# The recurrence's level products and solve in all four quadrants, with VectorE's order of work rearranged

## The reference, cut to what matters

```python
sa = einsum('bhvk,bhk->bhv', S, a_t)
S  = S * w_t + sa[..., None] * b_t + v_t[..., None] * k_t
y_t = einsum('bhvk,bhk->bhv', S, r_t)
```

## Time and profile before

| what | us |
|---|---|
| median of 3 runs | 1070.66 (1070.43 to 1071.26) |
| the profiled execution | 1070.18 |
| its span | 1068.4 |
| PE busy | 1039.6 (97%) |
| VectorE busy | 653.9 (61%) |
| ScalarE busy | 453.0 (42%) |

### The profile page before, as it was taken

The page is one execution under the profiler, slowest core; times in us unless marked ns, Lnnn a source line. Parts: engine busy times, 40 slices in busy tenths (PEclk is TensorE's granted clock), DMA queues, the critical chain, the costliest instruction groups (busy, mean ns, idle before and its releaser), DMA issues.

```text
span 1068.4 us, 22579 instructions
## 1 busy us (share of the span) xinstructions
PE 1039.6 (97%) x9816; PEld 823.4 (77%) x9816; DVE 653.9 (61%) x1025; ACT 453.0 (42%) x732; POOL 5.6 (1%) x10
## 2 busy tenths in 40 slices
PE   7999999999999989999999999999999999999998
PEld 5777777676777777777777767787888888888887
DVE  4569999977466665868677667664443223444322
ACT  5455555686335533443535245344432112443111
POOL 0000000000000000000000000000000000000000
PEclk9999999999999999999999999999999999999999
DMA  9912224000532110110110121322222232223230
GB/s 360 377 61 99 79 81 176 1 2 2 197 118 79 60 42 22 43 42 25 39 42 22 42 81 43 124 93 99 99 99 99 99 99 88 93 96 114 89 104 30
DMA packets 26161, 95.01 MB, mean 89 GB/s; under 512 B 2896, under 2 KB 3152, under 8 KB 25552
## 3 DMA queue, kind: packets, MB, share of 16 engines
q1 hardware_dynamic: 26064, 93.57, 25.1%
HBM read 89.36 MB, written 4.19 MB: 88 GB/s over the span
## 4 chain that ended last, share of the span: by engine, by line
PE 76%; DVE 16%; ACT 4%; issue 2%; DMA 1%; SPq 1%; POOL 0%; ACTq 0%; DVEq 0%
PE psum L857 19%; PE psum L858 18%; PE psum L859 18%; DVE work L2067 5%; PE psum L867 3%; PE psum L1310 2%; PE psum L1323 2%; DVE small_temps L2218 1%; PE psum L1045 1%; PE psum L1024 1%; PE psum L1359 1%; PE psum L1382 1%; DMA work<-weights 1%; DVE in_weights_low L2123 1%; PE psum L1110 1%
## 5 line engine op out<-in xcount | busy, mean ns | idle before, releaser
L2123 DVE TENSOR_TENSOR weights_low<-ring,weights_high 128x1024 fp32r<-128x1024 f32 x70 | 85.8, 1226 | 75.3 <-ACT weights_high L1673 75.3
L1673 ACT ACTIVATE weights_high<-ring 128x1024 fp32r<-128x1024 f32 x70 | 73.6, 1052 | 127.5 <-PE psum L859 127.5
L857 PE MATMUL psum<-normed_high,weights_high 128*128 128x512 f32 x256 | 100.2, 391 | 0.2 <-DVE weights_low L2123 0.2
L859 PE MATMUL psum<-normed_high,weights_low 128*128 128x512 f32 x256 | 99.7, 389 | 0.0
L859 PE MATMUL psum<-hidden_high,weights_low 128*128 128x512 f32 x256 | 99.7, 389 | 0.0
L858 PE MATMUL psum<-normed_low,weights_high 128*128 128x512 f32 x256 | 99.6, 389 | 0.0
L858 PE MATMUL psum<-hidden_low,weights_high 128*128 128x512 f32 x256 | 99.6, 389 | 0.0
L857 PE MATMUL psum<-hidden_high,weights_high 128*128 128x512 f32 x256 | 99.6, 389 | 0.0
L2067 DVE SCALAR_TENSOR_TENSOR work<-work,small_sb 128x512 f32<-128x512 f32 x116 | 80.2, 745 | 0.2
L1643 ACT ACTIVATE work<-psum 128x384 f32<-128x384 f32 (+1 forms) x110 | 54.1, 541 | 56.3 <-PE psum L1359 18.8
L857 PE MATMUL psum<-pair_normed_high,pair_weights_high 128*128 128x512 f32 x176 | 75.8, 431 | 0.8 <-DVE normed_low L2127 0.8
(11 more groups left out here) (320 smaller groups left out, 2102.6 us busy)
## 6 DMA issues: line engine op xcount, KB each, us to landing
ring<-weights SPq DMA_DIRECT2D x135, 512.0 KB, 3.7
work<-weights SPq DMA_DIRECT2D x10, 512.0 KB, 12.9
residual<-xT SPq DMA_DIRECT2D x4, 512.0 KB, 7.1
mixed<-weights SPq DMA_DIRECT2D x4, 512.0 KB, 7.8
residual_saved<-residual SPq DMA_DIRECT2D x8, 256.0 KB, 4.4
residual<-residual_saved SPq DMA_DIRECT2D x1, 2048.0 KB, 9.0
outT<-residual SPq DMA_DIRECT2D x8, 256.0 KB, 3.3
tables_sb<-tables SPq DMA_DIRECT2D x1, 1280.0 KB, 10.4
```

The costliest lines, as they stand in the source:

```text
L857: pe.matmul(out, wh, high(k), start=first and n == 0, stop=False)
L859: ins = pe.matmul(out, wl, high(k), start=False, stop=last and n == len(order) - 1)
L1673: act.activation(wsplit(q)[0], room_of(b), ACT.Copy).then_inc(w_high, 1)
L2123: vec.tensor_tensor(low, room_of(b), high.bitcast(F32), ALU.subtract).then_inc(w_low, 1)
```

## The change

The products of both heads of a level are issued together for the levels in `CROSSED`, head 1 into the half of its bank that head 0 doesn't write, so that four quadrants are in use; the first level is left as it was. `solve` does the same. What head 1 finds in the other half is put right by VectorE: `Y` of head 1 is written by two instructions of 64 partitions each, and `WU` of head 1 is copied out by two VectorE instructions in place of one of ScalarE. `times_inverse_both` and `solve` wait for both heads' earlier steps before they start. VectorE's steps for other pairs get new places. The plan of PSUM banks and all other PE work is unchanged.

```diff
@@ -83,6 +83,7 @@
 STEPS = NQ * QT
 MTILES = S // P
 MUNITS = 2 * MTILES
+CROSSED = (4, 8, 16, 32)
 MU_AMID, MU_BEHIND = {0: 0, 1: 2, 2: 3, 4: 5}, {0: 1, 3: 4}
 MU_SOLVE = len(MU_AMID) + len(MU_BEHIND)
 MU_CHAIN = MU_SOLVE + 1
@@ -1302,6 +1303,18 @@
                         if c == G - 1:
                             full_inc(ins, name)
 
+            def times_inverse_both(p, b):
+
+                names = [f"y{b}_{p}_{h}" for h in range(HEADS)]
+                outs = [take(name, G * C).rearrange("p (c t) -> p c t", c=G) for name in names]
+                for c in range(G):
+                    for q in range(PARITIES):
+                        for h in range(HEADS):
+                            ins = pe.matmul(outs[h][rows(q ^ h), c, :], NT[rows(1 - q), h, c, :],
+                                            XN[rows(1 - q), h, c, :], start=True, stop=True)
+                            if c == G - 1:
+                                full_inc(ins, names[h])
+
             def times_inverse(name, h):
 
                 out = take(name, G * C).rearrange("p (c t) -> p c t", c=G)
@@ -1351,15 +1364,16 @@
                             if (c, h) == (G - 1, HEADS - 1):
                                 full_inc(ins, f"mv_{p}")
 
-            def solve(p, h):
-
-                out = take(f"wu_{p}_{h}").rearrange("p (c n) -> p c n", c=G)
+            def solve(p):
+
+                outs = [take(f"wu_{p}_{h}").rearrange("p (c n) -> p c n", c=G) for h in range(HEADS)]
                 for c in range(G):
                     for q in range(PARITIES):
-                        ins = pe.matmul(out[rows(q), c, :], XT[rows(q), h, c, :], TAM[rows(q), c, h, :],
-                                        start=True, stop=True)
-                        if c == G - 1:
-                            full_inc(ins, f"wu_{p}_{h}")
+                        for h in range(HEADS):
+                            ins = pe.matmul(outs[h][rows(q ^ h), c, :], XT[rows(q), h, c, :], TAM[rows(q), c, h, :],
+                                            start=True, stop=True)
+                            if c == G - 1:
+                                full_inc(ins, f"wu_{p}_{h}")
 
             def transitions(p):
 
@@ -1436,7 +1450,10 @@
                             pe.wait_ge(x_first, p + 1)
                         else:
                             pe.wait_ge(*is_free(f"x{prev}_{p}_{h}"))
-                        times_inverse(f"y{b}_{p}_{h}", h)
+                        if b not in CROSSED:
+                            times_inverse(f"y{b}_{p}_{h}", h)
+                    if b in CROSSED:
+                        times_inverse_both(p, b)
 
                     if p == NP - 1:
                         if b == LEVELS[0]:
@@ -1483,7 +1500,7 @@
                     pe.wait_ge(*is_free(f"ta_{p}"))
                     pe.wait_ge(*is_free(f"mv_{p}"))
                     pe.wait_ge(*is_free(f"xf_{p}_{h}"))
-                    solve(p, h)
+                solve(p)
                 if p + 1 < NP:
                     for x, lo, hi in BESIDE_CHAIN[0]:
                         project_part(beside_chain(p, x), lo, hi)
@@ -2004,8 +2021,7 @@
                 if p == NP - 1:
                     act.wait_ge(*is_free(f"gg_{NP - 2}"))
                     mixed_high(NP - 2)
-                for h in range(HEADS):
-                    copy_out(f"wu_{p}_{h}", WU[:, :, h, :], src=bank(f"wu_{p}_{h}").rearrange("p (c n) -> p c n", c=G))
+                copy_out(f"wu_{p}_0", WU[:, :, 0, :], src=bank(f"wu_{p}_0").rearrange("p (c n) -> p c n", c=G))
                 if p + 2 < NP:
                     pair_inputs(p + 2)
                 else:
@@ -2598,13 +2614,16 @@
                     mean_rest(p - 1)
                 late = p + 1 if p and p + 1 < NP else None
                 for b in LEVELS:
-                    if p + 1 < NP and b == LEVELS[2]:
-                        pair_input(p + 1, "v")
                     for h in range(HEADS):
                         name = f"y{b}_{p}_{h}"
                         vec.wait_ge(*is_full(name))
-                        free_inc(vec.tensor_tensor(Y[:, h], bank(name, G * C).rearrange("p (c t) -> p c t", c=G),
-                                                   mask(f"m{b}", G), ALU.mult), name)
+                        y, m = bank(name, G * C).rearrange("p (c t) -> p c t", c=G), mask(f"m{b}", G)
+                        if h == 0 or b not in CROSSED:
+                            ins = vec.tensor_tensor(Y[:, h], y, m, ALU.mult)
+                        else:
+                            for half in range(2):
+                                ins = vec.tensor_tensor(Y[rows(half), h], y[rows(1 - half)], m[rows(1 - half)], ALU.mult)
+                        free_inc(ins, name)
 
                     if p == NP - 1 and b == LEVELS[0]:
                         gn_centre(p - 1)
@@ -2618,13 +2637,8 @@
                     if late and b == LEVELS[1]:
                         changed_key(late)
                     if p + 1 < NP:
-                        if b == LEVELS[2]:
-                            unit_key(p + 1)
+                        if b == LEVELS[3]:
                             bonus_rest(p + 1)
-                        if b == LEVELS[3]:
-                            decayed_a(p + 1)
-                        if b == LEVELS[4]:
-                            decayed_b(p + 1)
                     for h in range(HEADS):
 
                         if b != LEVELS[-1]:
@@ -2642,6 +2656,8 @@
                     if late and b == LEVELS[1]:
                         decayed_r(late)
                         weights_after(late, "r")
+                    if p + 1 < NP and b == LEVELS[2]:
+                        pair_input(p + 1, "v")
                     if norm_late(p - 1):
                         if b == LEVELS[0]:
                             gn_centre(p - 1)
@@ -2656,18 +2672,22 @@
                         memory_unit(MU_BEHIND.get(LEVELS.index(b)))
 
                     if p + 1 < NP and b == LEVELS[3]:
-                        scaled_b(p + 1)
+                        unit_key(p + 1)
                         bonus(p + 1)
                 def by_pair(x):
                     return x.rearrange("p (c q) t -> p q c t", q=PARITIES)
 
                 if p + 1 < NP:
+                    decayed_a(p + 1)
+                    scaled_b(p + 1)
+                vec.wait_ge(*is_full(f"wu_{p}_1"))
+                wu = bank(f"wu_{p}_1").rearrange("p (c n) -> p c n", c=G)
+                for half in range(2):
+                    ins = vec.tensor_copy(WU[rows(half), :, 1, :], wu[rows(1 - half)])
+                free_inc(ins, f"wu_{p}_1")
+                if p + 1 < NP:
+                    decayed_b(p + 1)
                     weights_after(p + 1, "v")
-                    if norm_late(p - 1):
-                        gn_finish(p - 1)
-                        gate(p - 1)
-                    if late:
-                        decayed_key(late)
                 else:
                     for m in range(PAIR_MIX):
                         weights_low(SPLIT_AT[f"mix{m}"])
@@ -2688,6 +2708,13 @@
                         memory_unit(MU_CHAIN + n - 1)
                     vec.wait_ge(*is_full(name))
                     free_inc(scaled_sum(H[:, n + 1, :], bank(name, C), ELC[p % 2][:, n:n + 1], FB[:, n, :]), name)
+                    if late and n == 1:
+                        decayed_key(late)
+                    if p + 1 < NP and norm_late(p - 1):
+                        if n == 2:
+                            gn_finish(p - 1)
+                        if n == 3:
+                            gate(p - 1)
                     if p == NP - 2 and n == G:
                         memory_queries(0)
                     if p == NP - 1 and n in MIXED_AT:
```

## The result

The changed kernel takes 1072.34 us (median of 20 runs, 1071.21 to 1075.67); the kernel before, run beside it, 1069.08 (20 runs, 1068.05 to 1071.26). The forecast was 1071.1, no change, with 1065 to 1077 as its range.

The account below looks back on a forecast made before the run. PE was taken as the bound, full because other work lies between dependent steps. Pairs -0.6 - 0.2 - 0.5 + 0.65 + 1.1 = +0.45 us on 1070.66 gave 1071.1, no change; range 1065 to 1077, own range 1068.9 to 1073.3.

Parts of the forecast that it names:

- pair 5: Last pair, without projections: VectorE's weight blocks come behind its copies, GT starts near 659.5, first state at 663.3; +1.1 us.
- level 32: unit_key and bonus stand between VectorE's adds and masks; -0.35 us in pairs 0 to 3, +0.4 in pair 4.
- What four quadrants save: On PE, a level product shrinks from 1.08 to some 0.62 us, saving 0.46; the solve to 0.96, saving 0.93.
- Rival 4: On PE, the quadrants do not overlap, losing 2.6 us in five pairs and 1.5 in the last: 1085.6; chance 0.03.
- What the halves cost: On VectorE, 0.46 us per step: head 0's mask and two halves take 1.34; the WU copies take 1.44.
- Rivals 1 and 3: VectorE's halves overlap like full-height instructions (1066.3, chance 0.22), or cost more than 0.42 us each (1076.6 at 0.60, chance 0.16).
- Level 8: In pairs 1 to 4 mv waits for the bank pair_input of v frees: 1.1 us longer; pair 0 minus 0.25.
- Rival 2: At level 8, mv is not held up: 1.3 us less in four pairs, 1065.9; chance 0.07.
- Level 4: PE-bound between projections: minus 0.46, plus 0.13 waiting for both adds, net minus 0.33 us; pair 0 plus 0.1.
- Level 16: Takes the floor of 3.64 us: +0.6 in pair 0, +0.15 in pairs 1, 2 and 4, -0.3 in pair 3.
- Solve to transitions: Solve saves 0.93 us on PE; VectorE's two copies end 0.25 after the six projections, costing +0.25.
- The moved steps at nothing: VectorE's norm's end, gate, decayed_key and others in new places cost 0; without cover 0.6 us a pair.

Follow-up runs that it names:

- the windows above: Pair 3 of the changed kernel with the norm's end, the gate and decayed_key put back behind the last level; ratio to before 1.0199.
- the one with the bank of its own: Changed kernel with the masked values (mv) of pairs 0 to 4 in PSUM bank 6; ratio to before 0.9977.
- the one with both remedies: Changed kernel with mv of pairs 0 to 4 in PSUM bank 6 and ScalarE copying both heads' W and U in pair 5; ratio to before 0.9957.
- that of 0.9990: The kernel of 0.9940 with the old solve, head by head in two quadrants, and ScalarE copying both heads' W and U; ratio to before 0.9990.
- the kernel of 0.9940: Changed kernel with mv in bank 6, ScalarE's copies in pair 5, and only levels 4 and 8 of pairs 1 to 4 crossed; ratio to before 0.9940.

## Why the prediction was right, and where not

The time fell into the range, and most of the mechanisms named are those found. The direction was missed: 3.3 us slower can be told from none, where "no change" was forecast. Two steps failed, pair 5 and level 32.

- *What four quadrants save*: right. 0.62 to the next work, as estimated. The solve took 1.04 instead of 0.96. Rival 4 is out. The rule behind it (the Trainium skill, TensorEngine Tiling (Array Packing), Restrictions and Gotchas) does not hold for these products, whose row tiles write different halves of a bank. Sixteen products of 128 columns over the whole array (`turn_pairs`, 527.11 to 529.00) take 118 ns each. If the two row tiles took turns, at most two products would run at a time, and the solve's, of 128 columns too, would come every 59 ns (an estimate, by half of those 118); they come every 33 (1.04 us for 32).
- *What the halves cost*: right. The first half starts 0.46 behind the full mask, each takes 0.43; the copies took 1.39 for 1.44. Rivals 1 and 3 are out for this step.
- *Level 8*: right, +1.0 for +1.1, and `mv`'s wait 1.34 for 1.5. Rival 2 is out; moving the one step alone gave the loss, two ways to avoid the wait took it away. In pair 0 it was -0.47 for -0.25. There VectorE's new order alone gave 1.03 (3.03 with no level crossed, for 4.06 before), and crossing took 0.56 back.
- *Level 4*: right, -0.32 to -0.37 for -0.33.
- *Level 16*: the floor of 3.64 was a little low. Pairs 2 and 3 took 3.74, pairs 0, 1 and 4 3.63, 4.03 and 3.96. In pair 1 head 1's update lasts 0.94 to the next work and not 0.63; in pair 4 PE stands still for 0.42 us ahead of L1339 (at 595.10), which the profile puts down to "issue". No step foresaw either.
- *Level 32*: wrong for pairs 0 to 3: nothing for -0.35, about 1.4 us in all. The mask was in time. But the second low-rank product takes the bank that the bonus (L2509) frees. The bonus stands behind the adds of level 16 in both kernels, and it ends 1.16 us behind the start of level 32's product (549.78 for 548.62), as it did before (1.18). PE's weight load for that product waits for it:
```profile
549.84 0.29 PEld L868 LDWEIGHTS psum<-work,small_sb 64*128 64x128 f32 x2 [0.29 <-DVE tables_sb L2509]
```
The low-rank products then take 1.64 us to the next work instead of 1.21 (550.28 to 551.49), and the 0.46 saved is lost there. I counted `unit_key` and `bonus` as VectorE's work only, and not that PE waits for the bonus. Pair 4, without those products, gave +0.38 for +0.4. This reading is from the trace; no run moved the bonus alone.
- *Solve to transitions*: right, -0.72 to -0.76 for -0.93 + 0.25 = -0.68.
- *The moved steps at nothing*: right in their new place. The fourth state sum comes 0.6 later in its chain, as forecast, and delays nobody; the first state is 0.08 later. But "frees nothing" was true only beside the wait of 1.97 us that before had there. In the changed kernel, with the copies in that stretch, the same steps put back cost over 4 us a pair. The "0.6 a pair" without cover is the price inside the chain, and no run took the cover away.
- *Pair 5*: the step that failed. +1.1 was forecast, +2.2 measured. The weight blocks behind the copies were seen. Not seen was that the row maxima behind them feed ScalarE's exponentials, behind which stands the copy that frees a bank for the second `two_terms`: PE waits 2.21 us. I followed VectorE to GT and not ScalarE's queue: GT was forecast near 659.5 and came at 659.71, in a pair that began 0.5 earlier, but the first state came at 664.05 and not at 663.3. And "levels 8 to 32 come out even" was wrong at level 8: +0.72, where `mv` also waits 0.8 us for ScalarE.

For pairs 0 to 4 I summed -0.6 - 0.2 - 0.5 + 0.65 = -0.65, wrote no pair off by more than 0.5, and the traces give -0.14. Part of that nearness is luck, since the two gaps of pair 2 hide 0.75 us. Without them the five pairs come to +0.6, which is 1.3 from the forecast: level 32 missed by 1.4 and level 16 by 0.9 (+1.64 for +0.75), while level 8 came out 0.7 better (+3.5 for +4.15). With the +2.2 of pair 5 the change costs 2.8 us by the traces, near the 3.3 of the medians.

The base was off too. The forecast was put on 1070.66, the median of three runs, and 20 runs put the kernel before at 1069.08. So the measured time is only 1.2 us above 1071.1, but the change itself was forecast as +0.45 and is +3.3. That 1072.34 also lies in the narrower range of 1068.9 to 1073.3 is luck: on the median of 20 runs this range would end at 1071.7.

## What to carry to other kernels

When a step is moved on one engine, follow the buffer that it frees to whoever takes it next: one statement between masks and adds instead of behind them was worth 0.5% of the whole kernel, while all four crossed levels together gave nothing there. Four quadrants pay where other work fills the dependent chain (levels 4 and 8 of pairs 1 to 4, the solve), and lose where the chain is bare and the exchange of halves costs 0.56 us on it. When a stall of one engine goes away, price the steps that lay in it anew, and the queues of the third engine that they feed.

## What the runs showed of the hardware

**A stall costs the clock too.** In the windows above PE is busy 0.72 of 3 us, at a granted clock of 1.00; the next 3 us are granted 0.50, the 1.2 GHz level, with PE busy all the time. A pair lost some 1.5 us in its chain to that, beside the 2.8 of the stall. The same came up once in pair 5 of three other kernels: in the one with the bank of its own, right behind `two_terms`'s wait of 2.21 us (0.52 from 655 to 658 us); in the one with both remedies (0.56 from 664 to 666) and in that of 0.9990 (0.50 from 668 to 670), both without so long a wait. Yet in after, with the same wait of 2.21 us, the clock stayed full. What decides between the two stays open.

**A gap with no waiter.** All 14 traces have one or two gaps of PE of 0.46 to 1.80 us in pair 1 or 2 that the profile puts down to "issue". The line number differs by kernel, but the step does not: they lie inside `key_products` of pair 2 (5 traces, 1.17 to 1.44 us) or inside `two_terms` (13 traces). In the kernel of 0.9940 (by form, 467 to 480 us) it is 1.4 us ahead of L1313, which is `key_products` there, in that of 0.9990 1.8 us inside `two_terms` (L1407):
```profile
L1313 PE MATMUL psum<-work 64*64 64x128 f32 x64 | 2.2, 274 | 1.4 <-issue 1.4
```
```profile
462.51 0.29 PE L1407 MATMUL psum<-work 64*64 64x64 f32 x5 [1.80 <-issue]
```
The start of pair 0, which no edit reaches, lies between 379.84 and 381.43 us in the 14 traces. A difference of such a size between two traces can be the gap or that stretch and nothing of the edit. The cause of neither was looked into.
